# Two-layer decoder step on one core: the second x tile turned inside the first unit, masks and activation tables loaded ahead, the last cache groups of layer a in slots that come free two groups sooner

## The chip, the cores and the metric

The kernel runs on one core of a Trainium2 chip. The core has a matrix engine (TensorE, PE in the profile, with PEld for its weight loads), a vector engine (VectorE, DVE), an activation engine (ScalarE, ACT), GpSimd (POOL) and SyncE (SP), which here issues all DMAs. The metric is device time in microseconds (us) of one execution, as the median of several runs.

## The reference, cut to what matters

One inference step of a decoder with two layers, for one prompt of 512 tokens and 8 sample sequences of 4 tokens, all in float32, model width 1024.

```python
def project_a(h, w_in, q_gain, k_gain, pos):          # layer a, dilated windows
    u = jnp.einsum('ntd,de->nte', h, w_in)            # 1024 -> 3*3*512 + 512
    q = rope(rms_norm(q, q_gain), pos); k = rope(rms_norm(k, k_gain), pos)
def layer_a_prompt(x, ...):   # three patterns (128,1), (512,4), (2048,16), banded attention
def layer_a_sample(x, bufs, ...):                     # scores and values against three caches
    cat = jnp.concatenate([bufs[g], new_rows], axis=1)
    states.append(cat[:, -min(win, L + T):])
def dilated_output(outs, lses, z, w_out):
    return jnp.einsum('nte,ed->ntd', o * jax.nn.silu(z), w_out)
# layer b: the same frame around compressed, selected and window attention (paged cache)
xp, xs = layer_b(layer_a(xp, xs))
```

Each layer is x + W_out(mixer(rms_norm(x)) * silu(z)). The outputs are both streams of x and the new caches.

## The kernel before, in words

The program is a row of stages, each a block with its own instruction list for every engine and a barrier of all engines at its end: project_a_stage, attend_a_stage (prompt), sample_a_stage, project_b_stage, attend_b_stage, sample_b_stage. Inside a stage the order on an engine is the order in which the Python code writes it; engines meet by semaphores.

**Projection.** The 544 tokens are four tiles of 128 and one of 32 sample tokens. Each x tile is turned by TensorE (`Rows.turn`, 8 transposes), and copied with the norm gain into `hT`: chunks 0 to 3 by VectorE (`copy_by_vector`), chunks 4 to 7 by ScalarE (`copy_by_scalar`). A unit is one tile times 512 columns of the weight: 8 products over the chunks k, which the trace shows as 16 matmuls. `Rows.ready` lets a unit of the first column wait for both copies. Before the first unit TensorE turns tiles 0 and 1; tiles 2 and 3 follow unit 0 and tile 4 follows unit 1. SP loads x tile 0, the front half of the first weight column (`pa_w_front`, k 0 to 3), x tile 1, the back half (`pa_w0`), and then the rest. ScalarE loads its activation table at its first instruction.

**Attention of layer a.** For each of 4 tiles and 4 head pairs: scores into PSUM, VectorE adds a mask table while it copies and takes the least value (L777), ScalarE takes Exp (L730), TensorE turns the probabilities and multiplies with the values. The mask tables lie in a tile of two halves; SP loads the first two at the stage's start (L627) and then the first cache groups. VectorE and ScalarE first keep the sample tokens' q, k, v and z (L707, L708, L749, L750).

**Sample tokens of layer a.** The caches come as 28 groups of 1 MB in a ring of slots. Slots 0 to 3 lie in `region`, where the weight columns of the projections lie too, the others in a tile of their own. Groups 0 to 13 (keys) are turned and multiplied, groups 14 to 27 (values) are multiplied (L972), with units of the prompt's output product (L985) between them. A group's load waits until the group before it in its slot is used up (`cache_slot`, `slot_before`). The last four groups lie in slots 4 to 7, so that both columns of layer b's weight can be loaded into `region` while the values are worked on. At the end, twice: `scale_out` (L1119), `turn_out` (L996), and `merge` (L1131) with 8 vector instructions, and then `sample_output` (L1003).

## Time and profile before

| | |
|---|---|
| median of 3 runs | 1230.58 us (1229.31 to 1232.0) |
| profiled execution | 1231.72 us, span 1229.9 us |
| PE busy | 1175.3 us, 96% of the span |
| DVE, ACT, POOL busy | 461.1, 395.7, 302.3 us |
| DMA | 197.61 MB, mean 161 GB/s |
| mean granted TensorE clock | 0.991 |

TensorE is busy for nearly the whole span, and no other engine for half of it. So the time is read as TensorE's work plus its gaps, and a gap is read by what ended it.

### The profile page before, as it was taken

How to read it: one execution, taken by the hardware profiler on the slowest of the kernel's cores; microseconds unless marked ns; L12 is line 12 of the kernel's file. 1: busy time of each engine (PE TensorE's matmuls, PEld its weight loads, DVE VectorE, ACT ScalarE, POOL GpSimd, SP SyncE). 2: the span in 40 equal slices, each digit the busy share in tenths (PEclk: the TensorE clock that was granted, in tenths of full speed). 3: DMA queues.
4: the chain of work that ended last, by engine and by line, in shares of the span. 5: the costliest groups of instructions: out<-in, count | busy, mean ns of one | idle time of the engine just before them, and what ended most of it. 6: DMA issues, size and time to landing. Idle time of an engine off the chain costs nothing. (4 is left out here: it accounts for less than half of the span.)

```text
span 1229.9 us, 20969 instructions
## 1 busy us (share of the span) xinstructions
PE 1175.3 (96%) x7934; PEld 763.5 (62%) x7934; DVE 461.1 (37%) x1205; ACT 395.7 (32%) x924; POOL 302.3 (25%) x418
## 2 busy tenths in 40 slices
PE   7999999999899999799999999999998999999998
PEld 4676676577577773354544657555557868686543
DVE  2333333000255651244222302676663363636410
ACT  4111111111366630132211423666663343424200
POOL 0666665000000000057523101545450000000000
PEclk9999999999999999899999999999998999999999
DMA  7333334476120699306668962302007856554801
GB/s 270 137 137 136 146 137 173 173 283 209 60 93 4 225 389 361 106 2 238 239 240 318 354 201 85 117 2 70 2 1 192 228 145 204 160 170 133 212 22 51
DMA packets 85885, 197.61 MB, mean 161 GB/s; under 512 B 9834, under 2 KB 37402, under 8 KB 84634
## 3 DMA queue, kind: packets, MB, share of 16 engines
q1 hardware_dynamic: 85786, 196.27, 47.2%
q8 instruction: 64, 1.05, 0.3%
q14 instruction: 35, 0.29, 0.1%
HBM read 185.56 MB, written 73.28 MB: 210 GB/s over the span
## 5 line engine op out<-in xcount | busy, mean ns | idle before, releaser
L464 PE MATMUL bank<-region,la_hT 128*128 128x512 f32 x640 | 282.6, 597 | 0.0
L464 PEld LDWEIGHTS bank<-region,la_hT 128*128 128x128 f32 x640 | 172.7, 274 | 92.8 <-issue 43.3
L1415 PE MATMUL bank<-region,lb_oT 128*128 128x512 f32 (+1 forms) x448 | 185.6, 569 | 0.4 <-DVE lb_oT L268 0.4
L1415 PEld LDWEIGHTS bank<-region,lb_oT 128*128 128x128 f32 x448 | 83.3, 190 | 87.5 <-issue 82.9
L1723 PE MATMUL bank<-cs_chunks_turned,region 128*128 128x252 f32 x512 | 121.8, 383 | 3.1 <-DVE cs_chunks_turned L1788 2.2
L1723 PEld LDWEIGHTS bank<-cs_chunks_turned,region 128*128 128x128 f32 x512 | 93.7, 192 | 17.4 <-DVE cs_chunks_turned L1788 4.6
L1788 DVE COPY cs_chunks_turned<-bank 64x512 f32<-64x512 f32 x64 | 43.7, 683 | 69.5 <-PE bank L1707 69.4
L1790 ACT ACTIVATE cs_chunks_turned<-bank 64x512 f32<-64x512 f32 x64 | 38.0, 593 | 95.5 <-PE bank L1707 95.3
L540 POOL TENSOR_TENSOR pa_swapped<-pa_normed,pa_tables 128x256 f32<-128x256 f32 (+1 forms) x60 | 50.2, 855 | 67.5 <-DVE pa_normed L555 67.5
L2134 POOL TENSOR_SCALAR ab_probs<-ab_probs,ab_rec,lb_gates 128x128 f32<-128x128 f32 (+3 forms) x96 | 58.3, 626 | 33.6 <-DVE ab_rec L2180 33.5
L495 ACT ACTIVATE pa_squares<-bank 128x512 f32<-128x512 f32 (+1 forms) x30 | 16.0, 533 | 154.3 <-PE bank L464 146.7
L2466 PE MATMUL bank<-region,lb_oT 128*128 128x512 f32 x128 | 55.9, 595 | 0.0
L2029 PE MATMUL bank<-lb_kT,lb_qp 64*128 64x512 f32 (+3 forms) x256 | 53.1, 494 | 1.8 <-PEq L164 1.4
L1831 POOL TENSOR_SCALAR cs_ms<-cs_ss 63x4 f32<-63x4 f32 x8 | 1.5, 187 | 212.6 <-DVE cs_ss L1842 212.6
L2104 ACT ACTIVATE ab_probs<-ab_probs,ab_low 128x128 f32<-128x128 f32 (+3 forms) x96 | 52.5, 551 | 0.0
L745 POOL TENSOR_TENSOR la_z<-la_z,aa_rec 128x512 f32<-128x512 f32 x4 | 4.2, 1044 | 187.4 <-DVE aa_rec L760 187.4
L2166 DVE CUSTOM_DVE_ANT_0 ab_probs<-bank,consts 128x128 f32<-128x128 f32 (+3 forms) x96 | 43.0, 486 | 16.6 <-PE bank L2029 16.6
L1468 ACT ACTIVATE pb_work<-bank 128x256 f32<-128x256 f32 (+3 forms) x25 | 10.8, 430 | 118.8 <-PE bank L1415 113.8
L547 DVE TENSOR_REDUCE pa_square_sum<-pa_squares 128x8 f32<-128x512 f32 (+1 forms) x30 | 18.1, 604 | 74.1 <-ACT pa_squares L495 74.1
L530 POOL TENSOR_TENSOR pa_rstd<-pa_mean_square,consts 128x8 f32<-128x8 f32 (+1 forms) x30 | 43.8, 1460 | 2.5
L1981 ACT ACTIVATE region<-bank 128x512 f32<-128x512 f32 (+3 forms) x64 | 27.8, 434 | 47.1 <-PE bank L2040 46.9
L2466 PEld LDWEIGHTS bank<-region,lb_oT 128*128 128x128 f32 x128 | 24.0, 190 | 30.1 <-issue 30.1
(341 smaller groups left out, 1790.2 us busy)
## 6 DMA issues: line engine op xcount, KB each, us to landing
region<-in_a_w_in SPq DMA_DIRECT2D x9, 2048.0 KB, 7.8
out_new_dil_s<-in_cache_dil SPq DMA_DIRECT2D x8, 2032.0 KB, 12.9
region<-in_b_w_in SPq DMA_DIRECT2D x6, 2048.0 KB, 8.5
region<-in_cache_dil SPq DMA_DIRECT2D x11, 1024.0 KB, 14.0
sa_cache<-in_cache_dil SPq DMA_DIRECT2D x9, 1024.0 KB, 11.7
lb_qp<-in_cache_nsa_paged SPq DMA_DIRECT2D x32, 256.0 KB, 4.3
region<-in_cache_nsa_paged SPq DMA_DIRECT2D x32, 256.0 KB, 4.2
sb_sel_keys<-in_cache_nsa_paged SPq DMA_DIRECT2D x64, 128.0 KB, 3.3
```

The costliest lines, as they stand in the source:

```text
L464: ins = nc.tensor.matmul(U[u.v % 3][:, :], permuted(hT[:, k, :], u.g, u.t), W[:, u.c % 2, k, :], start=(k == 0), stop=(k == KC - 1))
L530: nc.gpsimd.tensor_tensor(rstd[:, i % 2, 0:H], ms[:, 0:H], S.const("half_power")[:, 0:H], ALU.pow).then_inc(s_rstd, 1)
L540: nc.gpsimd.tensor_tensor(o3[:, :, lo:lo + HALF], n3[:, :, HALF - lo:DH - lo], tab, ALU.mult).then_inc(s_sw, 1)
L1415: ins = nc.tensor.matmul(U[u.v % 3][:, 0:n], hT[:, k, u.t * P:(u.t + 1) * P], weight_rows(u, k), start=(k == 0), stop=(k == KC - 1))
L1723: ins = nc.tensor.matmul(self.hidden_bank(y)[:, 0:KVH * nb], self.w1[:, kv, off, mm, :], self.chunksT[:, y % 2, :, mm, off:off + nb], star ...
L1788: nc.vector.tensor_copy(dst, src).then_inc(self.s_ev[0], 1)
L1790: nc.scalar.activation(dst, src, ACT.Copy).then_inc(self.s_ev[1], 1)
L2029: nc.tensor.matmul(SC[u][:, 0:b.N], QP[b.j][part, 1, g, own_q], KT[part, 1 if b.win else 0, b.j, 0:b.N], start=True, stop=True).then_inc(s ...
L2104: nc.scalar.activation(slots[i][:, 0:b.N], slots[i][:, 0:b.N], ACT.Exp, bias=low[:, i:i + 1], scale=-1.0, accum_out=den[:, i:i + 1]).then_ ...
L2134: nc.gpsimd.tensor_scalar(slots[i][:, 0:b.N], slots[i][:, 0:b.N], rec[:, i:i + 1], GATES[:, b.t, at:at + 1], ALU.mult, ALU.mult).then_inc( ...
L2166: nc.vector.tensor_tensor_reduce(slots[i][:, 0:b.N], SC[u][:, 0:b.N], S.const("causal")[:, (TILES - 1 - b.t) * P:], -SCALE, 3e38, ALU.add, ...
L2466: ins = nc.tensor.matmul(B[6 + v % 2][:, :], oT[:, k, t * P:(t + 1) * P], W_out[:, k, half * 512:half * 512 + 512], start=(k == 0), stop=( ...
```

## The change

It has five parts. In both projections TensorE turns x tile 1 between the front and the back half of unit 0, and a unit of the first column waits for the vector engine's copy before k = 0 and for the activation engine's copy before k = 4. ScalarE runs a one-column Square at the start of the kernel and a one-column Exp at the start of layer a's attention. The first mask table has a tile of its own, which SP loads during the projection. The last four cache groups go to slots 2 to 5; layer b's second weight column, which lies over slots 2 and 3, is now loaded after they are used. `merge` does 2 vector instructions for 8.

```diff
-    def ready(self, pe, t):
-        pe.wait_ge(self.s_by_vector, t + 1)
-        pe.wait_ge(self.s_by_scalar, t + 1)
+    def ready(self, pe, t, k):
+        pe.wait_ge(self.s_by_scalar if k else self.s_by_vector, t + 1)
 # project_a_stage, SP: behind all other work of the stage
+                a = S.where["prompt_mask"][0]
+                sp.dma_start(first_table[:, :], A["consts"][:, a:a + 6 * P]).then_inc(S.lasting_sem("aa_first_masks"), 16)
 # TensorE
                 turn_x(0)
-                turn_x(1)
                 for u in units:
-                    if u.c == 0:
-                        rows.ready(pe, u.t)
...
                         elif u.v == 0 and k == 4:
+                            turn_x(1)
                             pe.wait_ge(s_w[0], 16)
+                        if u.c == 0 and k % 4 == 0:
+                            rows.ready(pe, u.t, k)
 # ScalarE
+                act.wait_ge(s_gt, 1)
+                nc.scalar.activation(sq[:, 0:1], S.const("ident")[:, 0:1], ACT.Square).then_inc(s_table, 1)
+                act.wait_ge(s_table, 1)
                 act.wait_ge(s_gc, 1)
                 x_tile(0)
                 x_tile(1)
 # attend_a_stage
-        tables = sb("tables", [P, 2, W0])
+        tables = [first_table, sb("tables", [P, W0])]
-                for t in range(TILES):
+                for t in range(1, TILES):
...
             def _(act):
+                nc.scalar.activation(spent[:, :], S.const("ident")[:, 0:1], ACT.Exp)
                 nc.scalar.activation(T.q[:, :, :, :], QK[:, 0:3, :, SEQ:TOK], ACT.Copy).then_inc(s_kept, 1)
 # sample_a_stage
 def cache_slot(m):
-    return m % SLOTS_A + (4 if m >= GROUPS_A - 4 else 0)
+    return m % SLOTS_A if m < GROUPS_A - 4 else 2 + m - (GROUPS_A - 4)
...
-                        for c in range(2):
-                            sp.wait_ge(s_pv, m - 8 + 2 * (c + 1) - NK)
-                            sp.dma_start(W_next[:, c, :, :], w[:, :, c * 512:(c + 1) * 512]).then_inc(S.lasting_sem(f"pb_w{c}"), 16)
+                        sp.wait_ge(s_pv, last_in(1) + 1 - NK)
+                        sp.dma_start(W_next[:, 0, :, :], w[:, :, 0:512]).then_inc(S.lasting_sem("pb_w0"), 16)
...
+                sp.wait_ge(s_pv, last_in(3) + 1 - NK)
+                sp.dma_start(W_next[:, 1, :, :], w[:, :, 512:1024]).then_inc(S.lasting_sem("pb_w1"), 16)
...
-                    for j in range(4):
-                        for e in range(2):
-                            part = slice(e * DH, (e + 1) * DH)
...
-                            nc.vector.tensor_tensor(dst, src, z, ALU.mult).then_inc(s_o, 1)
+                    step = P + 2 * NT
+                    for e in range(2):
+                        part = slice(e * DH, (e + 1) * DH)
+                        src = S.wide[2][part, 0:4 * step].rearrange("p (j s) -> p j s", s=step)[:, :, 0:P].rearrange(
+                            "p j (n c) -> p j n c", n=4)[:, :, :, e * NT:(e + 1) * NT]
...
+                        nc.vector.tensor_tensor(dst, src, z, ALU.mult).then_inc(s_o, 1)
 # project_b_stage, TensorE
                 rows.turn(pe, 0)
-                rows.turn(pe, 1)
...
+                        if u.v == 0 and k == 4:
+                            rows.turn(pe, 1)
+                        if u.c == 0 and k % 4 == 0:
+                            rows.ready(pe, u.t, k)
```

TensorE at the start of the program, in the kernel before. `consts,x` is the turning of an x tile, `region,la_hT` are the products of a unit, one row entry for each k; `s_x0` to `s_x2` are the landings of the x tiles.

```order
L256 MATMUL bank<-consts,x 128x128 [waits s_x0]
L256 MATMUL bank<-consts,x 128x128 x7
L256 MATMUL bank<-consts,x 128x128 [waits s_x1]
L256 MATMUL bank<-consts,x 128x128 x7
L464 MATMUL bank<-region,la_hT 128x512 [waits pa_w_front,pa_x_by_scalar,pa_x_by_vector]
L464 MATMUL bank<-region,la_hT 128x512 x3
L464 MATMUL bank<-region,la_hT 128x512 [waits pa_w0]
L464 MATMUL bank<-region,la_hT 128x512 x3
L256 MATMUL bank<-consts,x 128x128 [waits pa_x_by_scalar,pa_x_by_vector,s_x2]
```

The same stretch in the changed kernel:

```order
L256 MATMUL bank<-consts,x 128x128 [waits s_x0]
L256 MATMUL bank<-consts,x 128x128 x7
L466 MATMUL bank<-region,la_hT 128x512 [waits pa_x_by_vector,pa_w_front]
L466 MATMUL bank<-region,la_hT 128x512 x3
L256 MATMUL bank<-consts,x 128x128 [waits s_x1]
L256 MATMUL bank<-consts,x 128x128 x7
L466 MATMUL bank<-region,la_hT 128x512 [waits pa_x_by_scalar,pa_w0]
L466 MATMUL bank<-region,la_hT 128x512 x3
L256 MATMUL bank<-consts,x 128x128 [waits pa_x_by_scalar,pa_x_by_vector,s_x2]
```

The front half of unit 0 stands ahead of the wait for x tile 1, and each half waits for one of the two copies.

SP at the end of layer a's sample stage, in the kernel before. `in_cache_dil` are cache groups (rows of 128x4x512 are whole groups, four rows of 128x1x512 make one), `in_b_w_in` are layer b's weight columns.

```order
L829 DMA sa_cache<-in_cache_dil 128x4x512
L831 DMA sa_cache<-in_cache_dil 128x4x512 x2
L900 DMA region<-in_b_w_in 128x8x512 x2
L831 DMA sa_cache<-in_cache_dil 128x4x512 x2
L836 DMA sa_cache<-in_cache_dil 128x1x512 x8
L160 UNCONDITIONAL_BRANCH
```

The same stretch in the changed kernel:

```order
L836 DMA sa_cache<-in_cache_dil 128x4x512
L838 DMA sa_cache<-in_cache_dil 128x4x512 x2
L910 DMA region<-in_b_w_in 128x8x512
L838 DMA region<-in_cache_dil 128x4x512 x2
L843 DMA sa_cache<-in_cache_dil 128x1x512 x8
L922 DMA region<-in_b_w_in 128x8x512
L160 UNCONDITIONAL_BRANCH
```

The second weight column moved from before the last four groups to behind them, and two of those groups now go into `region`.

## Rows read from the trace of the kernel before

**Rows 1.** The page, part 1: busy time of each engine.

```profile
PE 1175.3 (96%) x7934; PEld 763.5 (62%) x7934; DVE 461.1 (37%) x1205; ACT 395.7 (32%) x924; POOL 302.3 (25%) x418
```

**Rows 2.** Timeline of PE at the start: start us, us, engine, line; [idle before].

```profile
5.30 1.97 PE L256 MATMUL bank<-consts,x 128*128 128x128 f32 x8 [1.86 <-DMA x<-in_x_prompt]
10.87 1.97 PE L256 MATMUL bank<-consts,x 128*128 128x128 f32 x8 [3.60 <-DMA x<-in_x_prompt]
12.62 7.63 PE L464 MATMUL bank<-region,la_hT 128*128 128x512 f32 x16
20.09 1.91 PE L256 MATMUL bank<-consts,x 128*128 128x128 f32 x16
21.84 7.03 PE L464 MATMUL bank<-region,la_hT 128*128 128x512 f32 x16
```

**Rows 3.** Line L204, load of the front half: issue and time to landing.

```profile
L204 SPq DMA_DIRECT2D region<-in_a_w_in x1: 434/434/434, 2.3 to 2.3; - x1
...
DMA to landing us min/median/max: 7.2/7.2/7.2
```

**Rows 4.** Timeline at the start of layer a's attention.

```profile
325.74 1.25 PE L674 MATMUL bank<-la_qk 64*128 64x512 f32 x4 [1.33 <-PEq L164]
...
327.41 0.20 DVE L750 COPY la_s_z<-la_z 128x128 f32<-128x128 f32 x1
329.16 0.96 DVE L777 CUSTOM_DVE_ANT_0 aa_probs<-bank,aa_tables 128x768 f32<-128x768 f32 x1 [1.55 <-DMA aa_tables<-in_consts]
...
330.21 1.28 ACT L730 ACT_TABLE_LOAD   x1 [3.56 <-DVE aa_low L777]
...
331.06 2.10 PE L674 MATMUL bank<-la_qk 64*128 64x512 f32 x4 [3.62 <-DVE aa_low L777]
...
335.94 1.25 PE L674 MATMUL bank<-la_qk 64*128 64x512 f32 x4
...
339.57 1.25 PE L674 MATMUL bank<-la_qk 64*128 64x512 f32 x4
```

**Rows 5.** Stretches: us, busy PE, PEld, DVE, ACT, POOL; granted clock, DMA share, GB/s.

```profile
332.00:333.00 1.00, 1.00 (x6) 0.38 (x4) 0.00 (x0) 1.00 (x3) 0.00 (x0) 0.50 0.31 117
...
508.90:510.00 1.10, 1.10 (x4) 0.71 (x4) 0.00 (x0) 0.00 (x0) 0.00 (x0) 0.50 0.00 0
```

**Rows 6.** Timeline at the end of layer a and the start of layer b.

```profile
490.73 1.07 PE L972 MATMUL bank<-sa_cache,sa_p_padded 128*32 128x512 f32 x8
...
496.49 7.32 SPq L836 DMA_DIRECT2D sa_cache<-in_cache_dil  x8
...
501.50 0.66 PE L996 MATMUL bank<-consts,sa_out 128*128 128x128 f32 x4 [0.45 <-DVE sa_out L1119]
502.09 2.78 PE L972 MATMUL bank<-sa_cache,sa_p_padded 128*32 128x512 f32 x24
...
506.96 1.06 PE L972 MATMUL bank<-sa_cache,sa_p_padded 128*32 128x512 f32 x8 [2.09 <-DMA sa_cache<-in_cache_dil]
...
508.90 1.12 PE L996 MATMUL bank<-consts,sa_out 128*128 128x128 f32 x4 [0.88 <-DVE sa_out L1119]
510.05 1.60 DVE L1131 TENSOR_TENSOR la_hT<-bank,sa_z_t 64x16 f32<-64x16 f32 x8 [1.21 <-PE bank L996]
511.71 3.64 PE L1003 MATMUL bank<-la_w_out,la_hT 128*32 128x256 f32 x32 [1.69 <-DVE la_hT L1131]
...
516.67 1.94 PE L256 MATMUL bank<-consts,x 128*128 128x128 f32 x16 [1.32 <-PEq L164]
...
517.34 0.69 DVE L268 TENSOR_TENSOR lb_oT<-bank,norm_gain_cols 128x512 f32<-128x512 f32 x1 [5.69 <-PE bank L256]
...
519.02 7.11 PE L1415 MATMUL bank<-region,lb_oT 128*128 128x512 f32 x16 [0.41 <-DVE lb_oT L268]
```

**Rows 7.** Timeline of PE at layer b's sample output.

```profile
1187.84 3.66 PE L2474 MATMUL bank<-region,lb_oT 128*32 128x256 f32 x64 [0.94 <-DVE lb_oT L2664]
```

**Rows 8.** Timeline of SP: layer b's third weight column, issued when its first column is done.

```profile
552.10 0.39 SPq L1269 DMA_DIRECT2D region<-in_b_w_in  x1
```

More of the change, by code:

```diff
@@ L124, in constants @@
     return np.ascontiguousarray(np.concatenate(flat, 1)), where
-LASTING = (["s_const", "s_ident", "s_gain_rows", "pa_w_front", "s_copy", "s_page_table", "pa_vout", "pb_rows_out", "pb_win_out", "pb_sample_rows_out", "oa_stored", "ob_stored",
+LASTING = (["s_const", "s_ident", "s_gain_rows", "pa_w_front", "aa_first_masks", "s_copy", "s_page_table", "pa_vout", "pb_rows_out", "pb_win_out", "pb_sample_rows_out", "oa_stored", "ob_stored",
             "pa_w0", "pa_w1", "pb_w0", "pb_w1", "pb_w_last", "cmp_w", "cmp_small", "cp_pages0", "cs_pages0", "cs_pages1", "oa_w", "ob_w"]
@@ L321, with project_a_stage @@
 LAG = 3
-def project_a_stage(S, hT, W, QK, V, Z):
+def project_a_stage(S, hT, W, QK, V, Z, first_table):
     nc, A = S.nc, S.dram
@@ L362, in project_a_stage @@
         s_order, s_ordered = S.sem("pa_x_order_stored"), S.sem("pa_x_ordered")
-        s_gt, s_gc = S.sem("pa_norm_gains_turned"), S.sem("pa_norm_gains_copied")
+        s_gt, s_gc, s_table = S.sem("pa_norm_gains_turned"), S.sem("pa_norm_gains_copied"), S.sem("pa_table")
         s_w = [S.lasting_sem(f"pa_w{i}") for i in range(2)]
@@ L593, in rope_tab, with attend_a_stage @@
     return tabs[:, which, part, u.set, :]
-def attend_a_stage(S, QK, V, Z, T, oT, ring, spare):
+def attend_a_stage(S, QK, V, Z, T, oT, ring, spare, first_table):
     nc = S.nc
@@ L605, in sb @@
             return ctx.enter_context(nc.sbuf_tensor("aa_" + name, shape, F32))
-        tables = sb("tables", [P, 2, W0])
+        tables = [first_table, sb("tables", [P, W0])]
+        spent = sb("table", [P, 1])
         own = sb("probs", [P, 5, W0])
@@ L610, in attend_a_stage @@
         probs = [own[:, i, :] for i in range(5)] + [spare[:, 0:W0]]
-        s_tab = [S.sem(f"aa_table{t}") for t in range(TILES)]
+        s_tab = [S.lasting_sem("aa_first_masks")] + [S.sem(f"aa_table{t}") for t in range(1, TILES)]
         s_sc, s_m, s_e, s_tr, s_pv, s_rec, s_zr, s_zt, s_zc, s_fin, s_kept = (
@@ L623, in _ @@
                 a = S.where["prompt_mask"][0]
-                for t in range(TILES):
+                for t in range(1, TILES):
                     if t >= 2:
                         sp.wait_ge(s_m, HA * (t - 1))
-                    sp.dma_start(tables[:, t % 2, :], S.dram["consts"][:, a + t * W0:a + (t + 1) * W0]).then_inc(s_tab[t], 16)
+                    sp.dma_start(tables[t % 2][:, :], S.dram["consts"][:, a + t * W0:a + (t + 1) * W0]).then_inc(s_tab[t], 16)
                     if t >= 1:
@@ L776, in mask @@
                         dve.wait_ge(s_sc, 2 * p + e + 1)
-                        nc.vector.tensor_tensor_reduce(probs[i], SC[e][:, 0:W0], tables[:, t % 2, :], -SCALE, 3e38,
+                        nc.vector.tensor_tensor_reduce(probs[i], SC[e][:, 0:W0], tables[t % 2][:, :], -SCALE, 3e38,
                                                        ALU.add, ALU.min, low[:, i:i + 1]).then_inc(s_m, 1)
@@ L889, in quad, with last_in @@
             return slice(32 * i, 32 * i + 32)
+        def last_in(slot):
+            return max(i for i in range(GROUPS_A) if cache_slot(i) == slot)
         with S.block() as block:
@@ L993, in turn_out @@
                     else:
-                        pe.wait_ge(s_o, 8)
+                        pe.wait_ge(s_o, 2)
                     for j in range(4):
@@ L999, in sample_output @@
                 def sample_output():
-                    pe.wait_ge(s_o, 16)
+                    pe.wait_ge(s_o, 4)
                     for k in range(4):
@@ L1123, in merge @@
                     dve.wait_ge(s_ztc, 1)
-                    for j in range(4):
-                        for e in range(2):
-                            part = slice(e * DH, (e + 1) * DH)
-                            h = 2 * j + e
-                            src = B[4][part, j * P:(j + 1) * P].rearrange("p (n c) -> p n c", n=4)[:, :, h * NT:(h + 1) * NT]
-                            dst = oT[part, j, SEQ + 16 * b:SEQ + 16 * (b + 1)].rearrange("p (n t) -> p n t", t=NT)
-                            z = zT[part, j, 16 * b:16 * (b + 1)].rearrange("p (n t) -> p n t", t=NT)
-                            nc.vector.tensor_tensor(dst, src, z, ALU.mult).then_inc(s_o, 1)
+                    step = P + 2 * NT
[3 more added lines that the diff above has]
+                            "p j (n c) -> p j n c", n=4)[:, :, :, e * NT:(e + 1) * NT]
+                        dst = oT[part, :, SEQ + 16 * b:SEQ + 16 * (b + 1)].rearrange("p j (n t) -> p j n t", t=NT)
+                        z = zT[part, :, 16 * b:16 * (b + 1)].rearrange("p j (n t) -> p j n t", t=NT)
+                        nc.vector.tensor_tensor(dst, src, z, ALU.mult).then_inc(s_o, 1)
                 pad(0)
@@ L1174, in layer_a @@
             Z = sb("z", [P, TILES + 1, WA], inner)
-            project_a_stage(S, hT, W, QK, V, Z)
-            attend_a_stage(S, QK, V, Z, T, oT, ring, region[:, 3 * 4 * WA:])
+            first_table = sb("first_masks", [P, 6 * P], inner)
+            project_a_stage(S, hT, W, QK, V, Z, first_table)
+            attend_a_stage(S, QK, V, Z, T, oT, ring, region[:, 3 * 4 * WA:], first_table)
         W_out = sb("w_out", [P, 4, D])
@@ L1393, in _ @@
                 rows.turn(pe, 0)
-                rows.turn(pe, 1)
                 for u in units:
                     n = cols[u.c][1]
-                    if u.c == 0:
-                        rows.ready(pe, u.t)
                     if u.first and u.c == NC - 1:
```

## The prediction

> **What bounds the kernel now.** I read the page's busy times first [rows 1]: TensorE works 1175.3 of 1229.9 us, 96% of the span, so only its 54.6 us of gaps and its stretches at the lower clock can be won. Then I went through TensorE's own timeline and kept the gaps that the change touches. There are four places. At the start TensorE stands still for 3.60 us until x tile 1 has landed [rows 2]. At the start of layer a's attention it stands for 3.62 us before its second row of scores (L674 at 331.06), and the vector engine, which it waits for, had itself waited 1.55 us for the mask table [rows 4]. At the end of layer a's sample tokens it waits 2.09 us for the last cache group (506.96), 0.88 us for the scaled output (508.90) and 1.69 us for the merge (511.71) [rows 6]. At the start of layer b it has 0.41 us [rows 6]. Last I read the granted clock of these places [rows 5]: 0.50, the 1.2 GHz level, at 332 and at 509, so behind two of these gaps TensorE also works at half speed. Outside such places its work is dense, and what a place gains should reach the end unchanged.
>
> **The start, part by part.** Before, unit 0 follows both turnings, at 12.62. Now its front half (8 of 16 matmuls) needs tile 0's vector copy, which is there by 8.0 at the latest (the turning ends at 5.30 + 1.97 = 7.27, a copy of this size takes 0.69 [rows 2, 6]), and the front half of the weight: issued at 2.3, landed 7.2 later, at 9.5 [rows 3]. So the weight decides: 9.6. Price of a matmul: 7.03 / 16 = 0.43 at the 2.4 GHz level (21.84 to 28.8) and 0.86 at half of it; 8 turnings are 0.96 (half of 1.91) and 1.97 when slow [rows 2]. From 12.62 to the next turning at 20.09 are 7.47 us where 16 x 0.43 = 6.88 would do; the 0.59 over are 1.4 matmuls at half speed, so the clock rose at about 12.6 + 1.2 = 13.8, some 2.9 us after the second turning began at 10.87. If it rises at the same moment, the front half has 4.9 matmuls done by 13.8, the other 3.1 take 1.3 (15.1), the turning 0.96 (16.1), the back half 3.44: 19.5, a gain of 0.6. If it rises 2.9 us after the work begins (12.5), the same sum gives 3.4 matmuls, then 2.0, 0.96, 3.44: 18.9, a gain of 1.2. If it rises only behind the inserted turning, the front half costs 6.9, the turning 1.97, the back half 3.44: 21.9, a loss of 1.8. I take +0.9, between the first two, since the dense stretch before and now are alike; the ends stay in the range. The early Square moves a table load of 1.28 (as in [rows 4]) to where ScalarE has nothing to do; its copies are now needed only for k = 4, so it is worth nothing itself.
>
> The trace's clock, read from its matmuls, rises at 13.8 in this one execution. The Trainium skill ("TensorE: Matmul & The Clock Gate", section "What's actually happening") says that this moment is not tied to the kernel's start and moves from run to run; by that the gain would be any of the sums above, a different one in each execution, and the dips at 332 and 509 could also fall elsewhere. One trace cannot show it; it speaks for the first rival below.
>
> **The attention's start.** With the table there, the first masking waits only for the vector engine's own copies, which end at 327.41 + 0.20 = 327.61; it began at 329.16. Gain 1.55, and TensorE's next scores come at about 329.5 [rows 4]. What is late next: those copies, then the masking itself, so 2.1 of the 3.62 us stay. The second part is the clock: from this row of scores to the next took 4.88 us (331.06 to 335.94) at 0.50 [rows 4, 5], and the following interval, at full clock, 3.63 (to 339.57): 1.25 more, if the shorter gap keeps the clock up. The rows speak both ways: after 1.33 idle, the scores at 325.74 took 1.25, the full rate [rows 4]; the 2.09 us gap at 505 with the 0.88 behind it ended at 0.50 [rows 5, 6]. I count half, 0.65; the bounds are 0 and 1.25. The table load for Exp (1.28) moves from 330.21, where only ScalarE stood behind it, to the stage's start. There it delays the keeping copies by 1.3 + a small Exp, to about 328.2, before the first mask is ready at 328.6, so it is covered; uncovered it would cost a few tenths. Sum: 2.2, between 1.5 and 2.8.
>
> The first table's load itself is issued behind the last value store of the projection, a whole column of units before its end; it is one more wait of nothing on SP.
>
> **The end of layer a.** Before, the last group could be issued only after the values of group 23, which stand just ahead of the turning at 501.50, and SP is busy with the last two groups' eight DMAs until 496.49 + 7.32 = 503.8 [rows 6]. Now group 27 waits for group 21, done at 490.73 + 1.07 = 491.8 [rows 6], some nine microseconds before that turning, and not behind the 2 MB of the second weight column. It has to come 2.09 earlier: the gap goes, 2.1. The values of 27 then end at about 505.9, the chain behind them stays: scale_out 0.88, turning, merge, output. Merge is 8 instructions of 16 columns, 1.60 together, 0.20 each; a vector instruction of 512 columns is 0.69 [rows 6], about 0.001 per column, so two of 64 columns are 2 x 0.25 = 0.5: gain 1.1. (Bounds: no gain if a read across two PSUM banks with this stride costs four times that; 1.2 at 0.20 each.) And the clock: the turning at 508.90 took 1.12 at 0.50 where its like at 501.50 took 0.66, 0.45 less [rows 5, 6]; the output took 3.64 for 32 matmuls, where layer b's, of the same shape, took 3.66 for 64 [rows 7], so 1.83, 1.8 less. With the 2.09 gone, gaps of 0.88, some 0.6 and 1.32 remain with work between them; I expect the full clock. Sum 2.1 + 1.1 + 0.45 + 1.8 = 5.45, of which 3.2 need no clock.
>
> The price is the second weight column: SP now waits for group 25 (about 504) and 2 MB have to land before layer b's second column begins. Layer b's first column ends at 552.1, where SP issues the third [rows 8], that is some 40 us after, and a 1 MB load from the busy start took 7.2 [rows 3]. Covered; nothing else is queued behind that wait but the end of the stage.
>
> **The start of layer b.** Before: both turnings 516.67 to 518.6, unit 0 at 519.02 [rows 6]. Now one turning (0.97), the vector copy from 517.34 to 518.03, front half at about 518.15, its 3.44, the other turning 0.96, 3.44: 526.0. Before: 519.02 + 16 x 0.43 = 525.9. Nothing won: the turning that was cover for the copy is now inserted work. ScalarE gets its second tile 4 us later, and its copies for the sample tokens with it, but the products that need those come two units (14 us) later. I take 0, with -0.5 to +0.4.
>
> **Sum.** 0.9 + 2.2 + 5.45 + 0 = 8.55 against the profiled execution's 1231.72 gives 1223.2. That execution lies 1.14 above the median of 1230.58; I take off half of it and say 1222.6.
>
> **The rivals.** (1) The clock still dips at both places, or elsewhere instead, and only the waits go: 0.6 + 1.55 + 3.2 = 5.35, so 1226.4, less 0.57: 1225.8. For it: gaps remain at both places, and a gap of 2.1 was followed by a dip. Against it: the one at layer a's end loses its largest gap. (2) The attention's gain is given back: the loop behind it runs at a pace set by masking and copies, and catches up to where it was; then 2.2 are missing: 1224.8. Against it: intervals of 3.63 with TensorE at work back to back. (3) The last groups are as late as before, because the transfers ahead of them, not the slot, set their landing; then 2.1 and the 2.25 of clock stay away: 1227.0. Against it: they have nine microseconds more. (4) Slower: the two turnings split by waits at layer b's start, after layer a's three gaps, leave TensorE at the half clock through its first units. Each unit then costs 16 x 0.43 = 6.9 more. It decides from 8.55 / 0.43 = 20 matmuls on, into the second unit; two whole units are 13.8 more, 1222.6 + 13.8 = 1236.4. Against it: before, with gaps of 1.32 and 0.41 there, the turnings at 516.67 took 0.12 each, the full rate [rows 2, 6].
>
> **How the numbers follow.** Forecast 68%, its own range 1220 to 1225 (start and attention at their ends, and where in 1229.31 to 1232.0 the runs before would have been); rival 1 14%, rival 2 9%, rival 3 5%, rival 4 3%, no effect 1%. The range 1219.5 to 1226.5 takes in the forecast's, rival 1 and rival 2 and leaves out less than two in ten. About 0.2%, 2.5 us, is what can be told from no change: faster is below 1228.1. All cases but rival 4 and no effect lie there, some of rival 3 at its edge: faster 0.93, within 0.2% 0.04, slower 0.03.
>
> **What would show it.** TensorE's first unit starts at 9.6 and its next two turnings come at 18.9 to 19.5. No wait for a table at the first masking, the second scores 2.1 us after the first end. No wait for a DMA in layer a's values, two vector instructions of about 0.25 in the merge, a granted clock of 1.00 at the sample output, which takes 1.8. Unit 0 of layer b ends about as long after its stage's start as before, 9.3 us. I am wrong if a DMA still ends a gap there, if the output keeps 3.6, or if the projection of layer b starts with more idle time than 0.6.

## The result and the profile after

The changed kernel takes 1221.43 us (median of 4 runs, 1221.03 to 1221.81), beside 1231.29 for the kernel before in the same session (1229.31 to 1232.73). The ratio is 0.9923, 95% interval 0.9911 to 0.9936: 0.77% faster, which is 9.5 us, with 7.9 to 11.0 as the interval; the two medians lie 9.9 us apart. The forecast was 1222.6, with a range of 1219.5 to 1226.5. The profiled execution after took 1221.68 us, its span is 1219.9; before it was 1229.9, so the two profiles differ by 10.0 us.

The page's busy time of TensorE after, beside [rows 1]:

```profile
PE 1173.0 (96%) x7934; PEld 763.1 (63%) x7934; DVE 458.9 (38%) x1193; ACT 395.7 (32%) x926; POOL 301.8 (25%) x418
```

With the same 7934 matmuls TensorE is busy 2.3 us less, and idle 46.9 us for 54.6, 7.7 less. This is not yet a split of the gain into waits and clock: at the start the kernel after works at the lower clock where the one before stood idle. By the places read below, the clock's part is 3.4 us (1.26 at the attention, 2.16 at the end of layer a).

The timeline of PE at the start, after ([rows 2] before):

```profile
8.07 5.82 PE L466 MATMUL bank<-region,la_hT 128*128 128x512 f32 x8 [0.75 <-DMA region<-in_a_w_in]
13.72 1.04 PE L256 MATMUL bank<-consts,x 128*128 128x128 f32 x8
14.60 3.60 PE L466 MATMUL bank<-region,la_hT 128*128 128x512 f32 x8
18.03 1.15 PE L256 MATMUL bank<-consts,x 128*128 128x128 f32 x9
```

The front half of unit 0 starts at 8.07, when its weight lands, not at 9.6, and the turning of tiles 2 and 3 comes at 18.03 instead of 20.09: 2.06 earlier, and earlier than the 18.9 to 19.5 of the forecast. The load of the front half is the same instruction at the same time as in [rows 3], but it landed in 5.7 us for 7.2:

```profile
DMA to landing us min/median/max: 5.7/5.7/5.7
```

The timeline at the start of layer a's attention ([rows 4] before); the masking is now L784, the scores L680, the early load of the Exp table L713:

```profile
323.64 1.28 ACT L713 ACT_TABLE_LOAD   x1 [0.86 <-PEq L164]
...
323.68 1.25 PE L680 MATMUL bank<-la_qk 64*128 64x512 f32 x4 [1.33 <-PEq L164]
...
325.34 0.20 DVE L757 COPY la_s_z<-la_z 128x128 f32<-128x128 f32 x1
...
325.50 0.96 DVE L784 CUSTOM_DVE_ANT_0 aa_probs<-bank,la_first_masks 128x768 f32<-128x768 f32 x1
...
327.40 1.25 PE L680 MATMUL bank<-la_qk 64*128 64x512 f32 x4 [2.03 <-DVE aa_low L784]
...
331.02 1.25 PE L680 MATMUL bank<-la_qk 64*128 64x512 f32 x4 [0.47 <-DVE aa_low L784]
```

The first masking waits for no table: it follows the vector engine's own copy (325.34 + 0.20 = 325.54). The wait before the second scores is 2.03 us for 3.62, the first interval of scores 3.72 us (327.40 - 323.68) for 5.32, the second 3.62 for 4.88. TensorE reaches the end of this attention, the first turning behind it (L915 before, L927 after), at these times, the first row before, the second after:

```profile
411.02 0.30 PE L915 MATMUL bank<-consts,la_s_z 128*128 128x128 f32 x1 [1.94 <-PEq L164]
```

```profile
406.07 0.30 PE L927 MATMUL bank<-consts,la_s_z 128*128 128x128 f32 x1 [1.92 <-PEq L164]
```

From the first scores that is 85.28 us before and 82.39 after: 2.89 shorter, all of it kept.

The timeline at the end of layer a and the start of layer b ([rows 6] before; the output is now L1015, the merge L1143, layer b's units L1429):

```profile
479.83 9.82 SPq L843 DMA_DIRECT2D sa_cache<-in_cache_dil  x8
...
496.80 0.66 PE L1008 MATMUL bank<-consts,sa_out 128*128 128x128 f32 x4 [0.45 <-DVE sa_out L1131]
...
499.37 0.37 SPq L922 DMA_DIRECT2D region<-in_b_w_in  x1
501.90 0.66 PE L1008 MATMUL bank<-consts,sa_out 128*128 128x128 f32 x4 [0.88 <-DVE sa_out L1131]
502.60 0.47 DVE L1143 TENSOR_TENSOR la_hT<-bank,sa_z_t 64x64 f32<-64x64 f32 x2 [0.75 <-PE bank L1008]
503.13 1.94 PE L1015 MATMUL bank<-la_w_out,la_hT 128*32 128x256 f32 x32 [0.56 <-DVE la_hT L1143]
506.37 1.07 PE L256 MATMUL bank<-consts,x 128*128 128x128 f32 x8 [1.31 <-PEq L164]
507.88 3.67 PE L1429 MATMUL bank<-region,lb_oT 128*128 128x512 f32 x8 [0.44 <-DVE lb_oT L268]
...
515.69 1.91 PE L256 MATMUL bank<-consts,x 128*128 128x128 f32 x16
...
541.83 0.38 SPq L1282 DMA_DIRECT2D region<-in_b_w_in  x1
```

SP issues the last groups until 489.7 (479.83 + 9.82) instead of 503.8, and no DMA ends a gap of TensorE here. Two merge instructions take 0.47 for eight in 1.60. From the first turning (496.80) to layer b's first turning (506.37) are 9.57 us; before they were 15.17. The second weight column, moved behind the groups, is issued at 499.37 and needed when the first is done, at 541.83. Layer b's first stretch, from its first turning to the one of tiles 2 and 3, takes 9.32 us (515.69 - 506.37). Before, that second turning came 9.29 us behind the first, at 516.67:

```profile
525.96 1.91 PE L256 MATMUL bank<-consts,x 128*128 128x128 f32 x16
```

Stretches of the profile after, columns as in [rows 5], for the second pair of the attention, the sample output and layer b's start:

```profile
327.40:331.00 3.60, 3.15 (x24) 2.44 (x24) 1.87 (x5) 1.96 (x6) 0.00 (x0) 1.00 0.44 170
503.20:505.00 1.80, 1.80 (x32) 0.86 (x32) 0.00 (x0) 0.00 (x0) 0.00 (x0) 1.00 1.03 400
506.30:516.00 9.70, 9.19 (x35) 5.09 (x36) 1.38 (x2) 5.68 (x16) 1.14 (x2) 1.00 0.05 14
```

The granted clock is 1.00 at all three. The whole difference of the two spans, by anchors on TensorE, is then

| stretch | gain, us |
|---|---|
| start, to the turning of tiles 2 and 3, and from there to the attention | 2.06 + 0.00 |
| layer a's attention | 2.89 |
| its sample tokens, to the first turning of their output | -0.25 |
| from the first turning of the sample output to the output | 3.88 |
| the output and the way to layer b | 1.72 |
| layer b | -0.27 |
| sum | 10.03 |

### The profile page after: what moved, and what is told of

It is laid out like the page before. It is cut to its first block and busy times, and to the rows that moved or that the text cites. A ratio compares the mean times of both kernels' runs of the same rounds, so it can differ in the third digit from the quotient of the medians.

```text
span 1219.9 us, 20957 instructions
## 1 busy us (share of the span) xinstructions
PE 1173.0 (96%) x7934; PEld 763.1 (63%) x7934; DVE 458.9 (38%) x1193; ACT 395.7 (32%) x926; POOL 301.8 (25%) x418
## 5 line engine op out<-in xcount | busy, mean ns | idle before, releaser
L1429 PE MATMUL bank<-region,lb_oT 128*128 128x512 f32 (+1 forms) x448 | 185.7, 569 | 0.4 <-DVE lb_oT L268 0.4
L1429 PEld LDWEIGHTS bank<-region,lb_oT 128*128 128x128 f32 x448 | 83.4, 190 | 86.9 <-issue 83.0
L1995 ACT ACTIVATE region<-bank 128x512 f32<-128x512 f32 (+3 forms) x64 | 27.7, 433 | 46.9 <-PE bank L2054 46.7
```

Source lines behind the costliest of these rows:

```text
L1429: ins = nc.tensor.matmul(U[u.v % 3][:, 0:n], hT[:, k, u.t * P:(u.t + 1) * P], weight_rows(u, k), start=(k == 0), stop=(k == KC - 1))
```

## The experiments

Each kernel is the one before or the one after with one edit, in one case with two. Times are medians with ratios to the kernel before in the same session; the profile of each is read by the same anchors. Difference between two kernels means difference of their ratios times 1231 us. After has 0.9923. An interval of a ratio is about 2 us to either side, so many of these differences rest on the traces.

**The start as before.** Both first turnings ahead of unit 0 again, and both copies waited for. The early Square stays, so no run shows it by itself.

```diff
                 turn_x(0)
+                turn_x(1)
...
-                            turn_x(1)
```

> The changed kernel with layer a's first unit as before: both x tiles turned ahead of it, both copies waited for. Theory (the order of the turnings made the gain at the start): the turning of tiles 2 and 3 comes back from 18.0 to about 20.0 us, the rest shifts with it, +1.4 to +2.1 us on the changed kernel's 1221.4. Rival (the two profiled executions differed by luck: the front half of the weight landed 8.0 instead of 9.5, the clock rose at 12.4 instead of 13.8): the order itself is worth the 0.6 that the sum gives with the clock's rise fixed, so +0.6.

Measured: 1222.88 us, ratio 0.9922 [0.9907, 0.9937], no difference from after that a time can show: it decides neither for the theory nor for the rival. The trace of this kernel at the start:

```profile
9.41 1.97 PE L256 MATMUL bank<-consts,x 128*128 128x128 f32 x8 [2.12 <-DMA x<-in_x_prompt]
11.17 7.88 PE L467 MATMUL bank<-region,la_hT 128*128 128x512 f32 x16
18.89 1.36 PE L256 MATMUL bank<-consts,x 128*128 128x128 f32 x11
```

Tile 1 landed at 9.41, not at 10.87 as in the profiled execution of before, and the third turning came at 18.89. The traces of thirteen kernels, all but the last one of this section and with the shifted one among them, give that moment, in us, beside the one at which the granted clock goes from 1.2 to 2.4 GHz:

| old order: rise | 12.14 | 12.86 | 13.08 | 13.83 | 13.89 | 14.87 | |
|---|---|---|---|---|---|---|---|
| turning | 18.48 | 18.89 | 18.97 | 20.09 | 19.40 | 19.81 | |
| new order: rise | 11.58 | 11.74 | 12.36 | 13.05 | 13.26 | 13.69 | 13.97 |
| turning | 17.66 | 17.70 | 18.03 | 18.40 | 18.57 | 18.70 | 18.86 |

In either order the turning comes about 0.5 us later per us of rise, and the new order is about 0.5 to 0.6 us earlier at the same rise (18.89 at 12.86 against 18.40 at 13.05; 19.40 at 13.89 against 18.86 at 13.97); the 20.09 of the kernel before is the late landing. So the order is worth about 0.56, and the other 1.5 us of the profiles' 2.06 belong to these two executions.

**The mask table loaded at the stage's start.**

```diff
-                for t in range(1, TILES):
+                for t in range(TILES):
```

> The changed kernel with the first mask table loaded at the start of layer a's attention again, Exp's table load still early. Theory (the landing of the masks cost 1.6, and the longer gap the clock another 1.3): the first masking waits about 1.5 us for a DMA, TensorE's gap is 3.6 us, the clock falls to 0.50 in it or behind it and the interval from the second to the third row of scores is near 4.9; +2.9 us. Rival (the early Exp table was what mattered for TensorE's next steps): the interval stays 3.6 and only the wait comes back, +1.5.

Measured: 1224.08 us, ratio 0.9936 [0.9918, 0.9954]. In its trace both parts are back: the wait before the second scores, and behind it the half clock.

```profile
324.50 1.25 PE L679 MATMUL bank<-la_qk 64*128 64x512 f32 x4 [1.33 <-PEq L164]
...
330.06 1.25 PE L679 MATMUL bank<-la_qk 64*128 64x512 f32 x4 [3.86 <-DVE aa_low L783]
...
334.64 0.82 PE L679 MATMUL bank<-la_qk 64*128 64x512 f32 x2
```

```profile
331.50:334.00 2.50, 2.50 (x16) 2.28 (x13) 2.02 (x5) 0.10 (x1) 0.00 (x0) 0.50 0.00 1
```

The intervals are 5.56 and 4.58 us for 3.72 and 3.62: 1.84 for the table and 0.96 for the clock. From the first scores to the turning behind the attention are 85.18 us, for 82.39 after and 85.28 before. The intervals of the two ratios overlap, so the sum, 2.8, rests on the trace. TensorE also waits 0.30 us at 433.2 and 1.27 us at 439.6 here, and the profile names nothing for it; such waits come up again with the filler.

**The filler.** The kernel before, wait and all, with 24 transposes whose results are unused in the gap before the second scores.

```diff
+                    if p == 0:
+                        for i in range(24):
+                            nc.tensor.transpose(T0[:, i % 4 * P:(i % 4 + 1) * P], ident, ident)
```

> The kernel before with 24 turnings of a constant on TensorE in the gap behind the first scores of layer a's attention (327.4 to 331.1); their result is not used. The wait for the mask table stays. Theory (the idle gap pulls the clock down): the clock stays at 1.00, the interval from the second to the third row of scores is 3.6 instead of 4.9, -1.25 us on the kernel before. Rival (the slow interval is ScalarE's table load or the late masks, not the clock): the interval stays 4.9, 0 us.

Measured: 1235.97 us, ratio 1.0049 [1.0035, 1.0063]: slower. At the place itself it does what theory said:

```profile
324.12 1.25 PE L674 MATMUL bank<-la_qk 64*128 64x512 f32 x4 [1.33 <-PEq L164]
...
325.75 2.84 PE L683 MATMUL bank<-consts 128*128 128x128 f32 x24
329.69 1.25 PE L674 MATMUL bank<-la_qk 64*128 64x512 f32 x4 [1.10 <-DVE aa_low L780]
...
333.31 1.25 PE L674 MATMUL bank<-la_qk 64*128 64x512 f32 x4
```

The table's wait stays (the interval is 5.57 us), but with TensorE at work in it the following interval is 3.62, not 4.88. In all five kernels with the table's wait and nothing in it the clock is at 0.50 in the second pair; in the eight without the wait and in this one with the filler it is 1.00 there. So the idle time, 3.62 to 3.86 us in the five, is what makes that dip, and all of the 1.25 belongs to it. The loss comes 100 us later, in waits of TensorE between 425 and 465 us for which the profile names nothing:

```profile
PE bank L947 <- issue: 4.1, 1, 4.1
PE bank L937 <- issue: 1.8, 1, 1.8
```

Neither the kernel before nor after has a wait without a name there. But at 440.0 and 435.2 us, close to where the filler's kernel waits 1.8, they wait 0.72 and 0.99 us, and the profile names ScalarE; the section on the hardware comes back to it.

**The same shift elsewhere.** To tell the filler's time from its place in the code, the kernel before with 24 tiny transposes (results unused) at the start, where TensorE is idle.

```diff
                 ins.then_inc(s_gt, 1)
+                for i in range(24):
+                    nc.tensor.transpose(U[1][0:KC, 0:KC], ident[0:KC, 0:KC], ident[0:KC, 0:KC])
```

> The kernel before with 24 tiny transposes (8x8, results unused) behind the turning of the norm gains, where TensorE is idle anyway until the first weights land. It sets apart two explanations of the 1.8 and 4.1 us stalls that the kernel with filler transposes in the attention's gap showed at 437 and 458 us with no wait named: (1) they come from where the later instructions stand in TensorE's instruction stream, which 24 more instructions move by the same distance here: the same two stalls appear, and the time is 1230.0 + 5 to 6 = 1235 to 1236 us; (2) they come from what the filler does in time (a different meeting of transfers and engines after the gap): no such stall, 1230.0 us within 1.5, and at most a little earlier clock rise at the start.

Measured: 1236.43 us, ratio 1.0039 [1.0025, 1.0054], and the same two waits at the same two instructions:

```profile
PE bank L946 <- issue: 4.2, 1, 4.2
PE bank L936 <- issue: 1.7, 1, 1.7
```

So the filler lost its gain by moving the code behind it, not by what it did in the gap.

**Slots as before, in the kernel after.**

```diff
-    return m % SLOTS_A if m < GROUPS_A - 4 else 2 + m - (GROUPS_A - 4)
+    return m % SLOTS_A + (4 if m >= GROUPS_A - 4 else 0)
```

> The changed kernel with the last four cache groups in slots 4 to 7 and both weight columns ahead of them, as before; the short merge stays. Theory (slots set the last group's landing, and its gap pulled the clock down): a wait of about 2.1 us for a DMA in the values comes back, the clock falls behind it, the output takes 3.6 instead of 1.9; +2.1 to +4.3 us. Rival (the clock fell because of all three gaps, the merge's above all): +2.1 alone with the output at 1.9.

Measured: 1226.00 us, ratio 0.9948 [0.9928, 0.9968], 3.1 us slower than after. The trace:

```profile
502.63 1.06 PE L983 MATMUL bank<-sa_cache,sa_p_padded 128*32 128x512 f32 x8 [1.91 <-DMA sa_cache<-in_cache_dil]
...
505.79 1.93 PE L1014 MATMUL bank<-la_w_out,la_hT 128*32 128x256 f32 x32 [0.57 <-DVE la_hT L1142]
```

The DMA's wait is back, 1.91 us, but the output runs at its full rate, 1.93: this gap by itself brought no dip in this trace.

**The long merge, in the kernel after.** The eight instructions of before in place of the two.

```diff
-                    for e in range(2):
+                    for j in range(4):
+                        for e in range(2):
```

> The changed kernel with the merge in 8 vector instructions; the new slots stay. Theory (the merge's price is its instructions): the wait before the output is 1.7 us instead of 0.6, +1.1 us, the output at 1.9. Rival (the longer merge pulls the clock down by itself): the output takes up to 3.6, +1.1 to +2.9 us.

Measured: 1223.05 us, ratio 0.9935 [0.9919, 0.9951], 1.5 us slower than after. From turning to output are 2.34 us in its trace for 1.23, so 1.1 as worked out; the output takes 1.93, so again no dip in this trace:

```profile
505.51 1.93 PE L1015 MATMUL bank<-la_w_out,la_hT 128*32 128x256 f32 x32 [1.69 <-DVE la_hT L1143]
```

**The new slots alone, in the kernel before.** The edit of the third experiment the other way round, with its two loads of layer b's weight.

```diff
-    return m % SLOTS_A + (4 if m >= GROUPS_A - 4 else 0)
+    return m % SLOTS_A if m < GROUPS_A - 4 else 2 + m - (GROUPS_A - 4)
```

> The kernel before with the new slots and weight order alone. Theory: the 2.1 us wait for the last cache group goes; the merge's gap of 1.7 stays, so the clock may or may not stay up at the output: -2.1 to -4.3 us on the kernel before. Rival (the transfers ahead of the groups, not the slots, set their landing): 0.

Measured: 1228.53 us, ratio 0.9988 [0.9979, 0.9997]: 1.5 us, with 0.4 and 2.6 as bounds. The DMA's wait goes (5.11 us between the turnings), yet the output takes 3.04, and behind it the clock is at 0.50:

```profile
506.79 0.66 PE L1001 MATMUL bank<-consts,sa_out 128*128 128x128 f32 x4 [0.88 <-DVE sa_out L1124]
509.13 3.04 PE L1008 MATMUL bank<-la_w_out,la_hT 128*32 128x256 f32 x32 [1.69 <-DVE la_hT L1136]
```

```profile
509.90:516.00 6.10, 4.80 (x36) 3.32 (x29) 0.69 (x1) 0.55 (x3) 0.95 (x1) 0.50 0.27 95
```

The gaps ahead of this output, 0.88 and 1.69, are those of the kernel with the long merge, whose output ran at full clock. Same instructions, same gaps, and the dip is in one trace and not in the other.

**Slots and merge together, in the kernel before.** Both edits, nothing else of the change.

```diff
+    return m % SLOTS_A if m < GROUPS_A - 4 else 2 + m - (GROUPS_A - 4)
...
-                    pe.wait_ge(s_o, 16)
+                    pe.wait_ge(s_o, 4)
```

> The kernel before with the two edits at the end of layer a together and nothing else of the change: the last four cache groups in slots that are free two groups sooner, and the short merge of the sample output (2 instructions a block for 8). It tests the largest term of the sum. Theory as predicted: 2.1 us of transfer wait, 1.1 us of merge wait and 2.25 us of half clock go together, 5.45 us: 1225.6 us beside 1231.0 of the kernel before, ratio 0.9956; in the profile the second turning follows the first by 5.1 us, the output follows by 1.2 us and takes 1.9 us at clock 1.00. Rival, from the single edits (slots alone gave 1.5 us, the long merge put back took 1.6): the waits go, 3.2 us, and the clock's part is not theirs, because the dip comes at another place: 1227.8 us, ratio 0.9974.

Measured: 1225.06 us, ratio 0.9961 [0.9947, 0.9974]: 4.8 us, with 3.2 and 6.5 as bounds. The trace has the end of layer a as after:

```profile
505.64 0.66 PE L1001 MATMUL bank<-consts,sa_out 128*128 128x128 f32 x4 [0.88 <-DVE sa_out L1124]
506.86 1.93 PE L1008 MATMUL bank<-la_w_out,la_hT 128*32 128x256 f32 x32 [0.57 <-DVE la_hT L1136]
```

The forecast 5.45 lies in the interval; 3.2, the waits without any clock, is at its edge. Beside the 1.5 for the slots alone, this suggests that a part of the clock's share comes with the two together; the two intervals do not show it.

**Layer b's order as before, in the kernel after.**

```diff
                 rows.turn(pe, 0)
+                rows.turn(pe, 1)
```

> The changed kernel with layer b's first unit as before, both x tiles turned ahead of it. Theory (the turning that covered the copy became work inside the unit, so nothing is won): no change from the changed kernel within 0.3 us; the first units' end lies as far behind the stage's start. Rival (the split waits cost or win at the first units): +0.5 or -0.5 us.

Measured: 1219.83 us, ratio 0.9924 [0.9909, 0.9938]: no difference from after. Layer b's first stretch is 9.33 us in its trace, for 9.32 and 9.29.

**No early Exp, in the kernel after.**

```diff
-                nc.scalar.activation(spent[:, :], S.const("ident")[:, 0:1], ACT.Exp)
```

> The changed kernel without the one-column Exp at the start of layer a's attention. Theory (the table load is beside the path): the load of 1.28 us comes back behind the first mask, the first Exp ends about 1.3 us later at 328.8, and TensorE, which turns the first probabilities at 329.0, waits a few tenths at most: +0 to +0.5 us. Rival (ScalarE's chain sets the next steps): +1.3 us.

Measured: 1221.14 us, ratio 0.9928 [0.9913, 0.9944], the intervals of scores 3.72 and 3.63, and the whole attention 82.39 us as in after: the early table load is worth nothing that shows.

**A version that waits less.** In the kernel after 2.03 us remain before the second scores. Here each half of a pair waits for the mask of its own bank only.

```diff
-                    if p:
-                        pe.wait_ge(s_m, 2 * p)
...
+                            if p and g == 0:
+                                pe.wait_ge(s_m, 2 * p - 1 + e)
```

> The changed kernel, except that the scores of a head pair no longer wait for both masked halves of the pair before them: each half's first score matmul waits only for the half whose bank it writes. In the changed kernel 2.03 us of idle TensorE time still stand between the first two pairs of layer a's attention. Theory: the second masked half is what ends that wait, the first half is ready some 0.5 to 0.7 us sooner (one mask step of the trace), and the scores of the first half run beside the second mask; the idle time falls to about 1.4 us, and in the later 15 pairs, where TensorE does not wait there, nothing changes: 1220.8 us beside 1221.4, ratio to the kernel before 0.9918. Rival: the wait moves whole to the second half of the same pair, because the half's score matmuls are shorter than the mask step; then the time stays at 1221.4.

Measured: 1221.04 us, ratio 0.9915 [0.9895, 0.9935]: the smallest ratio of all, 1.0 us below after's, and the intervals overlap. In the trace the second scores wait 1.15 us for 2.03:

```profile
326.89 1.70 PE L680 MATMUL bank<-la_qk 64*128 64x512 f32 x3 [1.15 <-DVE aa_low L784]
```

The whole attention is 0.41 us shorter than after (81.98 from first scores to the turning behind it). So it beats the kernel before, and after perhaps by some tenths, which the medians do not show.

**Warming TensorE up.** The kernel after with 6 full transposes (results unused) in the idle time before the first x tile.

```diff
+                for i in range(6):
+                    nc.tensor.transpose(U[1][:, i % 4 * P:(i % 4 + 1) * P], ident, ident)
```

> The changed kernel with 6 filler transposes (128x128, results unused) behind the turning of the norm gains, in the 1.7 us in which TensorE is idle until the first x tile lands. Over the traces so far the turning of tiles 2 and 3 begins about 0.5 us earlier per us by which the clock rises earlier. Theory: the clock goes up some 1 to 2 us sooner and the first units run faster: 0.5 to 1 us, 1220.6 us, ratio 0.9916. Rival: the rise is not tied to when the engine begins (it moved between 11.58 and 13.97 us in the six traces of this order with no edit there), so nothing is gained: 1221.4. Second rival: the filler shifts the instructions behind it by 12 and a stall without a named wait appears later, some us slower.

Measured: 1223.11 us, ratio 0.9941 [0.9920, 0.9962]. The clock rose at 11.74 and the third turning came at 17.79, among the values of the kernels without filler (11.58 to 13.97; 17.66 to 18.86): nothing to be seen. Waits without a name came instead, 1.4 and 0.5 us:

```profile
PE bank L937 <- issue: 1.4, 1, 1.4
PE bank L967 <- issue: 0.5, 1, 0.5
```

## Why the prediction was right, step by step

The sum was 8.55 us; the profiles differ by 10.03, the medians by 9.9. The kind of each gain was as forecast, and three of the sizes were off. That the total came so near is in part luck: most of what the two profiles show at the start, and the full size of the clock's part at the end of layer a, do not come back in other traces.

**The start, 0.9.** The mechanism held: the front half runs on tile 0 while tile 1's turning waits its turn. The size failed where I took +0.9 "between the first two" sums: the first of them, the rise at the same moment, gave 0.6, and the thirteen traces show about 0.56. The profiles' 2.06 hide this, because the landing at 9.5 on which "the weight decides: 9.6" rested was late in that one execution (7.2 us, for 5.6 to 5.9 in the thirteen other traces), and so was tile 1's. The rise wandered between 11.58 and 14.87 us, over much of the same range in both orders. The Trainium skill's page "TensorE: Matmul & The Clock Gate", section "What's actually happening", says that this moment does not depend on when the kernel starts and varies by about half a microsecond. The traces agree that it moves, but by 3.3 us.

**The attention, 2.2.** The table's 1.55 was 1.60 in the profiles (5.32 to 3.72) and 1.84 with the table put back. The clock's 0.65, "I count half", was the mis-sized term: 1.26 in the profiles, 0.96 with the table back, and the dip stands in five kernels of five with the wait, in none without it or with work in it. The two rows that I weighed, 1.33 idle without a dip and 2.09 with one, did not tell which way 2.03 at this place would go; only the other kernels did: seven have that gap of 2.02 or 2.03, and the clock stays at 1.00 in all of them. The early Exp, at nothing, was right.

**The end of layer a, 5.45.** 5.60 in the profiles: DMA 2.09 and merge 1.13 (1.69 to 0.56 of waiting), turning 0.46 and output 1.70 are 5.38 of it, the rest are differences of a tenth. The waits come back one by one when an edit is undone. The 2.25 of clock is the mis-sized term here. It is in the profile, but not tied to these gaps alone: three kernels end layer a as before does (before itself, the filler, the shifted one), and the output took 3.64 us in the first and 1.93 in the other two. With the DMA's wait or the long merge put into the kernel after it also took 1.93, and with the new slots and the long merge in the kernel before it took 3.04. What these gaps cost in clock on average no run settles; for both edits the median gave 4.8, with 3.2 and 6.5 as bounds.

**Layer b, 0.** Right: 9.29, 9.32, 9.33. The second weight column, 499.37 for 541.83, is covered.

**The rivals.** The first, only the waits with the clock dipping elsewhere instead, is half true: dips remain in each trace after, at other places (920 and 1135 in that of the kernel after, 508 in that of the half masks), but the attention's is gone. Had it been true whole, 5.35 would have come, and 9.9 did. The second fell: the attention kept its 2.89. The third fell: no DMA ends a gap behind 492 us. The fourth fell in its size: in the kernel after the clock is 1.00 from 506.3 to 516, and no whole unit ran slow in any trace. A small form of it is there in three of the eight traces with the new order in layer b: with the table at the stage's start, the half masks and the warm start, the first half unit runs at 0.50 for a while and takes 5.37 us for 3.67. In the four traces with the old order in layer b whose sample output ran at full clock (the kernel after with layer b as before, filler, shifted, slots and merge together) this does not come; so few traces do not show that the order brings it.

The 0.57 taken off for the execution was near the 0.43 by which its 1231.72 stands above the new median of the kernel before, 1231.29. What is not settled is the -0.25 in the sample tokens and the -0.27 in layer b: they lie within what a dip more or less makes in a single trace.

**What the medians say.** Undone one by one in the kernel after, the parts give -0.1 (start), 1.6 (table), 3.1 (slots), 1.5 (merge), 0.1 (layer b) and 0.6 us (Exp), 6.8 in all, for a whole of 9.5; each is uncertain by some 2 us, so the rest is not placed. Most of that uncertainty is the clock, since the time of a run goes with its mean granted clock (see the section on the hardware). A straight line through the 133 runs whose clock is known, with one slope for all kernels (0.7 us for each thousandth of the clock) and a level for each kernel, gives an estimate of the differences at equal clock: 6.2 us between before and after, so that some 3.5 of the whole are clock; 1.5 for the table put back, 2.4 for the old slots, 0.6 for the long merge and 0.1 for the old start, each give or take about 0.9. That fits the 1.55, 2.1, 1.1 and 0.56 that the traces give for the waits.

## What to carry over

A wait of TensorE can cost itself and a stretch at half clock behind it, so read the granted clock behind each gap before the gap is priced; but count on only what comes back in the trace of another kernel. Price a reordering at the start by several traces: landings and the rise of the clock move by more than such an edit is worth. And before filling a gap with idle work, remember that added instructions move all code behind them: the waits that this brings can be larger than the gap.

## What the runs showed of the hardware

**Waits without a name.** The 24 fillers cost 4.8 to 6.0 us, at the start as in the gap, through two waits of 1.7 to 1.8 and 4.1 to 4.2 us at the same two instructions, in a stretch in which the data queues move some 385 GB/s. In the shifted kernel:

```profile
438.46 0.63 PE L936 MATMUL bank<-sa_keys_turned,sa_q_padded 128*32 128x128 f32 x12 [1.66 <-issue]
...
460.11 0.27 PE L946 MATMUL bank<-la_hT,sa_q_padded 128*32 128x32 f32 x7 [4.16 <-issue]
```

The profile names no releaser, but the traces point at the loading of TensorE's own instructions. The fourteen traces have ten such waits of over 0.1 us, in six kernels. Count all of TensorE's instructions in the trace up to each wait: it stands behind number 5313, 5569 or 5570, 6338 or 15553, each a multiple of 256 plus 193 or 194. And each ended 1.28 to 1.61 us after a 16 KB transfer of the instruction queue (q8 on the page, 64 such transfers beside some 16400 instructions) had landed. The kernels before and after wait at the same place, number 5570, and also 1.44 and 1.61 us after such a landing:

```profile
440.01 0.66 PE L923 MATMUL bank<-consts,region 128*128 128x128 f32 x4 [0.72 <-ACT sa_keys_turned L1034]
```

```profile
435.23 0.65 PE L935 MATMUL bank<-consts,region 128*128 128x128 f32 x4 [0.99 <-ACT sa_keys_turned L1046]
```

ScalarE, which the profile names there, had ended its copy 0.5 and 0.8 us earlier. The kernel with the table at the stage's start waits there too, 1.27 us, though its TensorE code is that of the kernel after. By these counts the place in the stream of instructions decides where TensorE can wait, and the moment of the transfer for how long; an added instruction moves other work to that place. No run moved the transfers alone, so the cause is strongly suggested and not proven, and why they come late in this stretch stays open.

The Trainium skill's page "Runtime: NRT & Kernel Launch", section "Instruction fetch mechanics", says that instructions are refilled in blocks of 256 and that crossing into the next is mostly hidden. The traces agree with both, in that the waits lie multiples of 256 apart and come at no more than two of some 64 blocks in any trace; but in the kernels with the 24 fillers these two cost some 5 us.

**The clock.** Besides the dip at the attention, which an idle wait of 3.62 to 3.86 us brings each time, stretches at the 1.2 GHz level come at other places from one kernel's trace to the next: some 20 us of them in all in that of the kernel before, some 10 in that of after. They go with the spread of the runs of one kernel over a few us: of the thirteen runs of the kernel before in the session of the half masks, the longest took 1234.46 us at a mean granted clock of 0.986, and the shortest 1228.45 at 0.995; the correlation of time and clock over the thirteen is -0.93.
